# A fused decoder layer on one core: product-key search decoded four heads at a time, some one-hots from ScalarE, expert rows from the third round

## Time and profile before

| | us |
|---|---|
| three runs: median | 2990.26 |
| lowest, highest | 2986.72, 2994.31 |
| profiled execution, its own time | 2988.07 |
| its span | 2986.2 |
| PE busy in the span | 2830.2 (95%) |
| DVE busy | 2320.3 (78%) |
| ACT busy | 1108.2 (37%) |
| POOL busy | 1160.0 (39%) |

### The profile page before, as it was taken

The page is one execution under the profiler, slowest core; times in us unless marked ns, Lnnn a source line. Parts: engine busy times, 40 slices in busy tenths (PEclk is TensorE's granted clock), DMA queues, the critical chain, the costliest instruction groups (busy, mean ns, idle before and its releaser), DMA issues. The chain is left out here.

```text
span 2986.2 us, 42826 instructions
## 1 busy us (share of the span) xinstructions
PE 2830.2 (95%) x15866; PEld 2537.2 (85%) x15866; DVE 2320.3 (78%) x4776; ACT 1108.2 (37%) x2079; POOL 1160.0 (39%) x878
## 2 busy tenths in 40 slices
PE   8997998999989999999999999989999999999997
PEld 7887886888979999999999999868888888888886
DVE  6114775567999998989997777488888888888887
ACT  3112332223222566666666767322222222222220
POOL 4113221002556544444445655144343434443431
PEclk9998999999999999999999999999999999999999
DMA  5224222222878777777778999799999999999991
GB/s 191 96 71 152 85 93 86 74 86 95 290 250 290 253 256 271 253 277 259 273 268 320 371 365 377 290 319 328 329 318 325 324 318 328 330 319 325 330 316 71
DMA packets 311483, 744.30 MB, mean 249 GB/s; under 512 B 22528, under 2 KB 136448, under 8 KB 308096
## 3 DMA queue, kind: packets, MB, share of 16 engines
q1 hardware_dynamic: 190976, 307.68, 31.1%
q0 software_dynamic: 92160, 335.59, 31.0%
q10 hardware_dynamic: 28160, 98.58, 8.3%
HBM read 623.26 MB, written 118.49 MB: 248 GB/s over the span
## 5 line engine op out<-in xcount | busy, mean ns | idle before, releaser
L1608 PE MATMUL y_ps<-v_hi,a_hi 128*128 128x512 f32 x1536 | 599.8, 391 | 20.3 <-DVE a_lo L1753 20.3
L1609 PE MATMUL y_ps<-v_lo,a_hi 128*128 128x512 f32 x1536 | 599.3, 390 | 0.0
L1610 PE MATMUL y_ps<-v_hi,a_lo 128*128 128x512 f32 x1536 | 598.9, 390 | 0.0
L884 POOL TENSOR_TENSOR u_lo<-u_raw,u_hi 128x1024 fp32r<-128x1024 f32 x128 | 306.6, 2395 | 604.5 <-ACT u_hi L880 603.4
L1207 PE MATMUL z_first<-hT_hi,u_hi 128*128 128x384 f32 x1024 | 358.8, 350 | 31.0 <-POOL u_lo L884 27.8
L1608 PEld LDWEIGHTS y_ps<-v_hi,a_hi 128*128 128x128 f32 x1536 | 289.4, 188 | 81.5 <-DVE a_lo L1753 21.0
L1208 PE MATMUL z_first<-hT_lo,u_hi 128*128 128x384 f32 x1024 | 349.3, 341 | 0.0
L1209 PE MATMUL z_first<-hT_hi,u_lo 128*128 128x384 f32 x1024 | 348.5, 340 | 0.0
L1610 PEld LDWEIGHTS y_ps<-v_hi,a_lo 128*128 128x128 f32 x1536 | 289.5, 188 | 60.4
L1609 PEld LDWEIGHTS y_ps<-v_lo,a_hi 128*128 128x128 f32 x1536 | 289.5, 188 | 59.8
L1249 ACT ACTIVATE late<-late 128x128 f32<-128x128 f32 x768 | 244.5, 391 | 177.7 <-DVE late L1376 157.9
(11 more groups left out here) (218 smaller groups left out, 6032.5 us busy)
## 6 DMA issues: line engine op xcount, KB each, us to landing
u_raw<-in_uT SPq DMA_DIRECT2D x128, 512.0 KB
room<-in_v SPq DMA_DIRECT2D x126, 512.0 KB
z<-z_sb ACTq DMA_DIRECT2D x128, 320.0 KB
gates<-late ACTq DMA_DIRECT2D x12, 2048.0 KB
gates<-g_sb ACTq DMA_DIRECT2D x12, 2048.0 KB
late<-gates SPq DMA_DIRECT2D x16, 1536.0 KB
room<-gates SPq DMA_DIRECT2D x15, 1536.0 KB
room<-z SPq DMA_DIRECT2D x16, 1280.0 KB
```

Source lines behind the costliest of these rows:

```text
L884: self.nc.gpsimd.tensor_tensor(self.u_lo[e][:], self.u_raw[e][:], self.u_hi[e][:].bitcast(F32), ALU.subtract).then_inc(self.u_lo_in[e], 1)
L1608: nc.tensor.matmul(o, ah, v_hi[p][:, i, c], start=(opens(r, s) and i == 0), stop=False)
L1609: nc.tensor.matmul(o, ah, v_lo[p][:, i, c], start=False, stop=False)
L1610: last = nc.tensor.matmul(o, al, v_hi[p][:, i, c], start=False, stop=(closes(r, s) and i == GROUP - 1))
```

## The change

Four edits, all in one diff:

1. **Decode for four heads.** `decode(link, b, first, n, near)` takes n heads. In the pieces of experts_in n is 4, so a block has two decodes instead of four, on 128x64 elements; their temporaries `step` and `past` lie in the PSUM bank `near`. The last head's decode of the blocks 0 and 1 still takes two heads, with temporaries in `near`. In the score stage nothing changes. `match` and `weigh` still take two heads, four times per block.
2. **Search spread.** The pieces come from a written list of 34: heads 0 to 3 with sides and pairs, the decode, heads 4 and 5 with the first matches and weighs between their pieces, heads 6 and 7, then the second decode and the last two matches and weighs. Decode, match and weigh are pieces of their own.
3. **Every fourth step's scaled one-hot by ScalarE from the index**, in turns 2 to 6 (40 of 192 steps): ACT computes abs(index - iota) and then relu(g - g * that) in 4 + 4 activations of 128x128, with a wait on its own semaphore between them. DVE makes only the other one-hot, half as wide. Per block DVE also writes -g, waiting first for ACT's last odd step of the block before. PE waits for `hot_in` beside `hot_g_in` in every step.
4. **Rows from the third round.** In experts_out the 320 row sets lie over rounds 2 to 30 instead of 1 to 30, evenly over all six blocks, and `start_block(0)` comes at the end of round 1 (n = 5).

```diff
-    def decode(self, link, b, two):
+    def decode(self, link, b, first, n, near=None):
...
+        pos = self.pos[:, b % 2, first:first + n]
+        row, col = self.ab[:, 0, 0:n], self.ab[:, 1, 0:n]
+        if near is None:
+            step, past = self.step[:, 0:n], self.past[:, 0:n]
+        else:
+            spare = near[:, NK + 5 * TOPK:NK + 13 * TOPK].bitcast(U32).rearrange("p (a h k) -> p a h k", a=2, k=TOPK)
+            step, past = spare[:, 0, 0:n], spare[:, 1, 0:n]
...
+        link(nc.vector.tensor_tensor(row, col, step, ALU.logical_shift_right))
+        link(nc.vector.tensor_tensor(past, row, step, ALU.logical_shift_left))
+        link(nc.vector.tensor_tensor(col, col, past, ALU.subtract))
...
+    PIECES = [(kind, h) for h in range(PH) for kind in (0, 1, "pairs")]
+    PIECES[12:18] = [("decode", 0), (0, 4), (1, 4), ("match", 0), ("pairs", 4), ("weigh", 0), (0, 5), ("match", 1), (1, 5),
+                     ("weigh", 1), ("pairs", 5)]
+    PIECES += [("decode", 1), ("match", 2), ("weigh", 2), ("match", 3), ("weigh", 3)]
...
+        def by_act(step):
+            return step // SLOTS < SIGNED and step % 4 == 3
...
                 def gates(step):
                     g = step % 2
+                    pe.wait_ge(hot_in[g], step // 2 + 1)
                     pe.wait_ge(hot_g_in[g], step // 2 + 1)
...
                 def scale_hot(step):
+                    if by_act(step):
+                        act.wait_ge(turned, step // SLOTS + 1)
+                        wait(act, g_done[g], step // 2)
+                        for t in range(4):
+                            last = nc.scalar.activation(hot[g][:, 0, t], iota[:], ACT.Abs, scale=-1.0,
+                                                        bias=iT[:, 0, i:i + 1])
+                        last.then_inc(apart, 1)
+                        act.wait_ge(apart, SLOTS // 4 * (step // SLOTS) + step % SLOTS // 4 + 1)
+                        for t in range(4):
+                            last = nc.scalar.activation(hot1_g[g][:, t], hot[g][:, 0, t], ACT.Relu,
+                                                        scale=minus_gT[:, i:i + 1], bias=gT[:, i:i + 1])
+                        last.then_inc(hot_g_in[g], 1)
+                        return
...
                 def make_hot(step):
+                    if by_act(step):
+                        nc.vector.tensor_tensor(hot[g][:, 1], bc(iota_ps, 1, 4), bc(iT[:, 1, t0:t0 + 4], 2, NK),
+                                                ALU.is_equal).then_inc(hot_in[g], 1)
...
                         if k == 1 and s >= FIRST:
                             v.wait_ge(found_T, s - FIRST + 1)
+                            wait(v, hot_g_in[1], SLOTS // 2 * (s - FIRST))
                             nc.vector.tensor_copy(iT[:], g_ps[0][:, 0:2])
+                            nc.vector.tensor_scalar(minus_gT[:], g_ps[0][:, 2], -1.0, None, ALU.mult)
...
         def rows_of(r):
-            return range(ROWS * max(r - 1, 0) // (NG - 2), ROWS * r // (NG - 2)) if r < NG - 1 else range(0)
+            return range(ROWS * max(r - 2, 0) // (NG - 3), ROWS * max(r - 1, 0) // (NG - 3)) if r < NG - 1 else range(0)
...
-                        if r == 1 and n == 1:
+                        if r == 1 and n == DB - 1:
                             v.wait_ge(rows_here, 16)
                             start_block(0)
```

More of the change, by code:

```diff
@@ L1073, in experts_in @@
     FIRST = TB - DB
+    SIGNED = DB - 1
     PRODUCTS_AT = [28, 28, 29, 29, 30, 31][:ZB]
@@ L1350, in keep_picked, with top_piece @@
                     nc.vector.engine_nop().then_inc(picked_in, 1)
[L1352 to L1360, removed]
[L1361 to L1370 removed]
+                def top_piece(b, kind, n):
+                    if kind == "decode":
+                        tk.decode(link, b, 4 * n, 4, near)
+                    elif kind == "match":
+                        tk.match(link, 2 * (n % 2))
+                    elif kind == "weigh":
+                        tk.weigh(link, b, n, near)
+                    elif kind == "pairs":
+                        tk.pairs(link, b, n, near)
+                        if n == PH - 1:
+                            tk.gaps(b).then_inc(gaps, 1)
+                    else:
+                        at = PH * (b - 2) + n
+                        x = at % 4
+                        if kind == 0:
+                            v.wait_ge(s_here[x], 16 * (at // 4 + 1))
+                        tk.side(link, kind, b, n, s_in[x][:, kind])
+                        if kind == 1:
+                            nc.vector.engine_nop().then_inc(s_taken[x], 1)
                 def make_hot(step):
@@ L1405, in last_head @@
                         tk.gaps(b).then_inc(gaps, 1)
-                        tk.decode(link, b, Q - 1)
+                        tk.decode(link, b, PH - 2, 2, near)
                     else:
-                        tk.match(link)
+                        tk.match(link, 0)
                         tk.weigh(link, b, Q - 1, near)
@@ L1494, in experts_out @@
         SKIP = UB - GB
-        DOTS_DONE = next(r for r in range(1, NG) if ROWS * r // (NG - 2) > dots[-1])
         HELD = (0, DB - 1)
@@ L1551, in rows_of @@
         def rows_of(r):
-            return range(ROWS * max(r - 1, 0) // (NG - 2), ROWS * r // (NG - 2)) if r < NG - 1 else range(0)
+            return range(ROWS * max(r - 2, 0) // (NG - 3), ROWS * max(r - 1, 0) // (NG - 3)) if r < NG - 1 else range(0)
+        DOTS_DONE = next(r for r in range(NG) if rows_of(r).stop > dots[-1])
         def spread(r, s):
-            mine, first = rows_of(r), 2 if r == 1 else 0
-            at = [len(mine) * max(k - first, 0) // (DB - first) for k in (s, s + 1)]
+            mine = rows_of(r)
+            at = [len(mine) * k // DB for k in (s, s + 1)]
             return mine[at[0]:at[1]]
```

51 lines of the change are left out of this document (24 added, 27 removed).

## The result

| | before, us | after, us |
|---|---|---|
| median | 2990.26 | 2937.28 |
| lowest, highest (5 runs of each) | 2986.72, 2994.31 | 2932.31, 2940.08 |
| ratio, 95% interval | | 0.9818, 0.9804 to 0.9831 |
| profiled execution, its span | 2988.07, 2986.2 | 2932.31, 2930.5 |

The gain is 53 us by the medians and 55.8 us by the profiled executions. The one profiled after is the fastest of its five. 2929 had been forecast, 8 us under the median and 3 us under the profiled execution; the range holds both.

What follows compares the result with a forecast made beforehand. DVE was taken to bound turns 0 and 1, PE and DVE nearly level in turns 2 to 5, and PE busy in experts_out except one hole. Terms 11 + 32 + 1 + 15 = 59 us, from 2988.1 to 2929; range 2905 to 2953.

Steps and rivals of the forecast that it cites:

- Turns 0 and 1, -11: In experts_in's turns 0 and 1, bound by DVE, DVE time saved on decodes shortens the stage by 11 us.
- Turns 2 to 5, -32: In turns 2 to 5, less DVE work and backlog shorten the stage by 32 us, ends 15 and 45.
- below the 12.4 that are lost: In turns 2 to 5, DVE's saving of about 8 us per turn counts, being under the 12.4 lost per turn.
- 3.4 of 3.8 us: hidden ... I take 0: ACT's own one-hot step after a tile's first half fits narrowly beside PE's work and costs 0.
- Rival B: ACT is late in its own steps, 20 us over turns 2 to 6: 2949 us; chance 0.15.
- It costs nothing in itself: The search spread in experts_in has the same pieces, 34 instead of 32, and no more waits: no cost.
- Turn 6, -1: In turn 6, eight steps with one-hots by ACT save 1 us, ends 0 and 4.
- experts_out, -15: In experts_out, moving rows out of round 1 closes PE's 13.85 us hole and saves 15 us, 12 to 17.
- rival D: Transfers bound experts_out: 1.8% more bytes per round cost 16 us in 29 rounds, 2945 us; chance 0.07.
- Rival E: ACT must reload tables for Abs and Relu between Gelus, 70 to 100 us: about 3015 us; chance 0.05.
- Rival C: The delay by POOL's u_lo moves wholly from decode to the match, 12.6 us back: 2942 us; chance 0.10.
- Rival A: DVE falls below PE throughout turns 2 to 5, clock recovers in turns 0 and 1: 2904 us; chance 0.15.

Runs made afterwards that it cites:

- e8: Kernel before with only the decode's temporaries moved to PSUM in experts_in, still two heads at a time: 2977.91 us, ratio .9961.
- e3: Kernel after with the decode's temporaries back in SBUF, still four heads at a time: 2943.30 us, ratio .9842.
- e4: Kernel after with each four-head decode done as two decodes of two heads at the same place: 2948.85 us, ratio .9864.
- e7: Kernel after with every second step's one-hot made by ACT instead of every fourth, in turns 2 to 6: 2941.00 us, ratio .9836.
- e2: Kernel after without one-hots by ACT; DVE makes both in all 192 steps and ACT only scales: 2940.84 us, ratio .9837.
- e5: Kernel after with decode, matches and weighs put into lumps, two neighbouring slots twice per turn: 2953.31 us, ratio .9880.
- e6: Kernel after with ACT's own one-hot steps in turns 2 to 5 only, not in turn 6: 2931.53 us, ratio .9803.
- e1: Kernel before with only the row sets moved to rounds 2 to 30 and start_block(0) at the end of round 1: 2974.38 us, ratio .9945.
- e1b: Kernel after with start_block(0) and its wait for h back at n = 1 of round 1, rows still from round 2: 2934.47 us, ratio .9813.

## Why the prediction was right or wrong

- **Turns 0 and 1, -11: right** (-12.3), and by the reason given: DVE stayed the bound, and what was taken from it was the stage's time. The terms: contention 4.8 of net gain, measured 5.8 by e8 (2.4 by e3); fewer decodes 6.0, measured 8.1 by e4. Of the latter, 1.6 us (17.7 - 16.1) is that the match is held up longer there, which the term did not have.

```profile
L836 DVE TENSOR_TENSOR room<-ab,places 128x1024 f32<-128x1024 uint32 x10 | 17.7, 1774 | 0.0
```

  That is e4's match in turns 0 and 1.
- **Turns 2 to 5, -32: right in sum (-30.8), wrong in its parts.** The step that failed is that DVE's saved time is the stage's as long as it is "below the 12.4 that are lost". For edit 3 15.8 us stood; it gave 11.4 at most, and the same again (e7) gave nothing. The other weak step is "3.4 of 3.8 us: hidden ... I take 0": ACT's step is 2.9 us, not 2.7, and the taking of the gates queued behind it, put at no cost, is what PE waits for (6.6 us). Rival B had PE wait for the own steps themselves, 20 us over turns 2 to 6; that is 1.2 us in turns 2 to 5, so B fell in its size. How much of the missing 4.4 us is ACT's stays open, as e2 shows. Edits 1 and 2 make up for it: without edit 3 the stage still fell by 19.4 us (e2), where 17.4 had been put down to edit 1. That the sum came within 1.2 us is partly luck.
- **"It costs nothing in itself" (edit 2): true, but it was given no price.** e5 shows that the layout matters, 17.2 us with the delay that came with it, and some 4 us are left for the spread by the estimate above. The text worked out that the backlog falls from 13.3 to 5.2 us, but used this only to confirm the 8.3 us per turn from the sum of work, and gave the spread no price. A backlog at the end of 28 slots doesn't show the worst moment within them. The kernel before has 16 waits in the earlier trace rows, four a turn: in the first of these turns they end at 1024.54, 1057.47, 1094.09 and 1127.21 us, one behind each slot with a decode, a match and a weigh.
- **Turn 6, -1: wrong, +3.3.** The step that failed is that less work for DVE there is a gain. DVE has none of it to lose: it waits for gathered rows. Waits of before and then of after in turn 6:

```profile
DVE u_rows L1388 <- DMA u_rows<-in_u,room: 17.1, 11, 5.0
...
DVE room L1388 <- DMA room<-in_u,room: 6.2, 8, 2.1
```

```profile
DVE room L1425 <- DMA room<-in_u,room: 19.6, 10, 7.6
DVE u_rows L1425 <- DMA u_rows<-in_u,room: 15.8, 8, 5.5
```

  23.3 us of waiting became 35.4, with 4.8 us more before for which no releaser is named; the DMA share is 0.96 before and 0.94 after. The same 62 row sets are asked for in any case. e6, without ACT's own steps there, waits 28.6 us and takes 150.7. Every kernel that has edit 4 reads 150.7 to 155.4 us here, and the two that haven't 148.4 and 148.8; but edit 4 touches no instruction of turn 6, so what makes the 2 to 7 us, the least of which are within what a stage varies by, stays open.
- **experts_out, -15: right** (-16.2). The hole was the rows' (e1), `start_block` and its wait for h cost nothing without the rows (e1b). The rounds did not get longer: PE is busy 962.00 of 962 us at a DMA share of 0.93, so rival D fell.
- **Rival E fell**: nine table loads as before. The Trainium skill, "ScalarE: Activation LUTs", section "Table sets: the hidden batching unit", has relu and abs in every set, and the trace agrees.
- **Rival C**, the delay moves to the match, is true for 9.3 of 20.6 us (e8), as the estimate had it. With four-head decodes it is 3.9 us, all in turns 0 and 1, and in turns 2 to 5 3.4 us moved on to L864, which the text had not named. **Rival A** fell: turns 0 and 1 stayed DVE's.
- **The end number** is 8 us under the median. 3 us of that are the terms above (59 against 55.8). The other 5 lie between the profiled execution and the median of the same kernel, on which the text had no term: it had seen 2.2 us of it before and left it out.

## What to carry to other kernels

Where a consumer is only a step or two behind, look also at the longest stretch of work in a row on the producing engine, and not only at its sum; and when the order of work is changed, look again at which operations meet another engine's, since e5's lumps cost 17.2 us of which most may be such a meeting. Before moving work to an engine that looks half idle, ask whether it is already a link of the same chain; the first quarter of the steps paid 11.4 of 15.8 us at best, the second quarter nothing. And a vector operation whose operands all lie in SBUF, beside GpSimd work of the same kind, is best given one operand in PSUM, each such operation in its turn, since the delay moves on to the next one that has none.

## What the runs showed of the hardware

- A 128x128 activation takes 390 to 391 ns as Copy or Abs, each with one operand per partition from a tile (Copy its scale, Abs its bias), and 484 ns as Relu with scale and bias both from tiles. Whether the function or the second pointer costs the 94 ns was not separated.
- Small vector operations on uint32 cost 0.19 us for 32 elements and 0.22 us for 64: half as many of twice the size save 40% of the time.
- The delay by GpSimd's `u_lo` picks its victims. In turns 2 to 5 of the kernel after no match is delayed (16 at 1.22 us), though `u_lo` runs 157.6 of 584 us, and in its place a short operation with two SBUF inputs is, which had 291 ns in the kernel before:

```profile
L864 DVE TENSOR_TENSOR found<-gap_e,gap_r 128x128 f32<-128x128 f32 x4 | 4.6, 1142 | 0.1
```

  Why the phase of the two engines falls so was not tried.
- Not every operation that lies in SBUF alone is delayed. In turns 0 to 5 of the kernel after the 96 MAX8 of `s_in` take 282 to 297 ns, while a Copy of 128x128 from SBUF to SBUF takes 229 ns to 2.31 us, and L824 of e3 0.18 to 2.40 us.
